# A hybrid retention and attention block: another order of slab products in head pairs 1 to 3

## The reference, cut to what matters

```
h    = rms_norm(x, norm1_g)
proj = h @ w_in                      # 2048 x 7168: rq rk rv rg aq ak av, 8 heads of 128 each
ret  = silu(rg) * group_norm(retention(rotary(rq), rotary(rk), rv))
att  = chunk_attention(rms_norm(aq), rms_norm(ak), av, rel_bias)
x    = x + concat(ret, att) @ w_out  # 2048 x 2048
x    = x + relu(rms_norm(x) @ w_ff1)^2 @ w_ff2      # d_ff = 8192
```

## Time and profile before

| what | value |
|---|---|
| median of 3 runs | 1123.92 us (1123.84 to 1124.09) |
| the profiled execution's own time | 1123.88 us |
| its span, first to last instruction | 1122.1 us |
| PE / DVE / ACT / POOL busy | 98% / 79% / 61% / 5% |
| mean granted TensorE clock | 0.998 |

### The profile page before, as it was taken

The page is one execution under the profiler, slowest core; times in us unless marked ns, Lnnn a source line. Parts: engine busy times, 40 slices in busy tenths (PEclk is TensorE's granted clock), DMA queues, the critical chain, the costliest instruction groups (busy, mean ns, idle before and its releaser), DMA issues.

```text
span 1122.1 us, 13185 instructions
## 1 busy us (share of the span) xinstructions
PE 1104.2 (98%) x5198; PEld 933.7 (83%) x5198; DVE 884.6 (79%) x881; ACT 688.3 (61%) x809; POOL 54.2 (5%) x66
## 2 busy tenths in 40 slices
PE   9799999999999999999999999999999999999998
PEld 9688888988988888888888888888888888888887
DVE  6878777777787768878788778788779788779784
ACT  6565565574565446668756568655667755577652
POOL 0100100100100000000000000000000000000000
PEclk9999999999999999999999999999999999999999
DMA  9785584585576556796797797797787797787792
GB/s 363 261 248 182 156 271 161 166 264 174 169 241 262 187 225 188 230 294 218 233 284 241 249 275 228 230 292 230 262 263 229 247 273 236 257 280 218 246 276 95
DMA packets 42958, 263.81 MB, mean 235 GB/s; under 512 B 4752, under 2 KB 6544, under 8 KB 15120
## 3 DMA queue, kind: packets, MB, share of 16 engines
q1 hardware_dynamic: 36704, 220.22, 52.6%
q0 software_dynamic: 5760, 41.95, 20.3%
q10 hardware_dynamic: 432, 0.81, 0.2%
HBM read 260.85 MB, written 2.10 MB: 234 GB/s over the span
## 4 chain that ended last, share of the span: by engine, by line
PE 85%; DVE 7%; ACT 3%; issue 2%; POOL 1%; ACTq 0%; DVEq 0%
PE acc L869 10%; PE acc L867 10%; PE acc L871 10%; PE acc L739 5%; PE acc L746 5%; PE acc L752 5%; PE bankC L829 4%; PE bankC L824 4%; PE acc L824 4%; PE acc L822 4%; PE bankC L822 4%; PE acc L829 4%; DVE w_lo L1403 3%; PE acc L591 2%; PE acc L596 2%
## 5 line engine op out<-in xcount | busy, mean ns | idle before, releaser
L1690 DVE TENSOR_TENSOR w_lo<-raw,w_hi 128x2048 fp32r<-128x2048 f32 x180 | 410.9, 2288 | 126.9 <-ACT w_hi L1206 126.7
L1206 ACT ACTIVATE w_hi<-raw 128x2048 fp32r<-128x2048 f32 x180 | 344.7, 1916 | 219.5 <-PE acc L871 145.5
L1403 DVE TENSOR_TENSOR w_lo<-raw,w_hi 128x1024 fp32r<-128x1024 f32 (+1 forms) x152 | 167.5, 1106 | 52.4 <-ACT w_hi L993 52.3
L993 ACT ACTIVATE w_hi<-raw 128x1024 fp32r<-128x1024 f32 (+1 forms) x152 | 143.1, 963 | 40.9 <-DVE raw L1412 32.5
L739 PE MATMUL acc<-w_hi,hT_hi 128*128 128x384 f32 (+1 forms) x416 | 105.5, 372 | 0.3 <-ACT w_hi L993 0.2
L867 PE MATMUL acc<-w_hi,hF_hi 128*128 128x512 f32 x256 | 100.8, 394 | 0.0
L871 PE MATMUL acc<-w_hi,hF_lo 128*128 128x512 f32 x256 | 99.7, 390 | 0.0
L869 PE MATMUL acc<-w_lo,hF_hi 128*128 128x512 f32 x256 | 99.7, 389 | 0.0
L746 PE MATMUL acc<-w_hi,hT_lo 128*128 128x384 f32 (+1 forms) x416 | 99.2, 356 | 0.0
L752 PE MATMUL acc<-w_lo,hT_hi 128*128 128x384 f32 (+1 forms) x416 | 98.9, 356 | 0.0
L867 PE MATMUL acc<-w_hi,dF_hi 128*128 128x512 f32 x248 | 96.9, 391 | 0.0
(11 more groups left out here) (262 smaller groups left out, 1813.8 us busy)
## 6 DMA issues: line engine op xcount, KB each, us to landing
raw<-in_w_up SPq DMA_DIRECT2D x64, 1024.0 KB, 6.2
raw<-in_w_down SPq DMA_DIRECT2D x64, 1024.0 KB, 6.1
raw<-in_w_ret SPq DMA_DIRECT2D x32, 1024.0 KB, 5.3
raw<-in_w_att SPq DMA_DIRECT2D x28, 768.0 KB, 4.2
raw<-in_w_out SPq DMA_DIRECT2D x16, 1024.0 KB, 4.9
raw<-in_w_up POOLq DMA_DIRECT2D x16, 1024.0 KB, 8.9
raw<-in_w_down POOLq DMA_DIRECT2D x16, 1024.0 KB, 8.6
raw<-in_w_ret POOLq DMA_DIRECT2D x8, 1024.0 KB, 8.5
```

Source lines behind the costliest of these rows:

```text
L993: nc.scalar.activation(piece(w_hi, q, 0, n), raw[:, r, half * n:(half + 1) * n], ACT.Copy).then_inc(hi_done, 1)
L1206: nc.scalar.activation(w_hi[:, ring(s)], raw[:, r, :], ACT.Copy).then_inc(slab_hi, 1)
L1403: nc.vector.tensor_tensor(piece(w_lo, q, 0, n), raw[:, IN_PLAN[i, READ_AT.get(step, step)][0], half * n:(half + 1) * n], piece(w_hi, q, 0, ...
L1690: nc.vector.tensor_tensor(w_lo[:, ring(s)], raw[:, r, :], w_hi[:, ring(s)].bitcast(f32), ALU.subtract).then_inc(slab_lo, 1)
```

## The change

Blocks 1 to 3 get another order of steps; block 0 keeps its order but some positions move; the x forms are made earlier on DVE; the first weight sum is put in front of the attention norm, on DVE and in POOL's queue; set_w no longer waits for set_y, but set_y for set_w. In order of pieces, blocks 1 to 3 after have I0 0-1, I1 2-3, I2 4-5, Q1 6-7, I3 8-9, J0 10-11, P5 12-13, J1 14-15, P6 16-17, J2 18-19, P7 20-21, J3 22-23, P3 24-25, and from Z1 on as before. No arithmetic is added or removed.

```diff
-STEPS = "I0 I1 I2 I3 J0 Q1 J1 P5 J2 P6 J3 P7 P3 Z1 Q2 Z2 P4 H1 H2".split()
-LOADS = "I0 I1 I2 I3 J0 a J1 b J2 d J3 Z1 e Z2 H1 H2".split()
+FIRST_STEPS = "I0 I1 I2 I3 J0 Q1 J1 P5 J2 P6 J3 P7 P3 Z1 Q2 Z2 P4 H1 H2".split()
+FIRST_LOADS = "I0 I1 I2 I3 J0 a J1 b J2 d J3 Z1 e Z2 H1 H2".split()
+STEPS = "I0 I1 I2 Q1 I3 J0 P5 J1 P6 J2 P7 J3 P3 Z1 Q2 Z2 P4 H1 H2".split()
+LOADS = "I0 I1 I2 a b I3 J0 d J1 J2 J3 Z1 e Z2 H1 H2".split()
...
+        def steps(i):
+            return STEPS if i else FIRST_STEPS
...
POOL:
-                att_power(2 * i)
                 pool.wait_ge(in_summed, 2 * i + 1)
                 add_ret(i, "b", 1, 1, in_b, i)
+                att_power(2 * i)
...
PE (att_T, att_scores, att_PT, att_pv):
-                for h, places in ((2 * i, (13, 15, 19, 21)), (2 * i + 1, (27, 28, 31, 33))):
+                first = (13, 15, 20, 22), (27, 28, 31, 33)
+                rest = (14, 16, 20, 22), (28, 30, 33, 34)
+                for h, places in zip((2 * i, 2 * i + 1), rest if i else first):
...
-                at_piece(i + 1, 5 if late else 7, ret_ZT, 2 * i + 1)
+                at_piece(i + 1, 5 if late else 8, ret_ZT, 2 * i + 1)
...
ACT:
             def set_y(i):
-                act.wait_ge(piece_used, in_first(i, "P7") + 2)
+                act.wait_ge(w_set, i + 1)
...
+                b = int(i > 0)
+                if b:
+                    at_piece(i, 8, keep_in_q1, i)
+                at_piece(i, (8, 10)[b], att_proj, h)
+                at_piece(i, (9, 11)[b], att_squares, h)
+                if not b:
+                    at_piece(i, 12, keep_in_q1, i)
+                at_piece(i, (16, 14)[b], keep_in_p5, i)
+                at_piece(i, (13, 14)[b], att_qT, h)
                 at_piece(i, 17, att_exp, h)
-                at_piece(i, 19, att_pT, h)
-                at_piece(i, 21, att_mix, h)
-                at_piece(i, 22, att_proj, h + 1)
-                at_piece(i, 23, set_y, i)
-                at_piece(i, 24, att_squares, h + 1)
-                at_piece(i, 25, set_h, i)
+                at_piece(i, 20, att_pT, h)
+                at_piece(i, 22, att_mix, h)
+                at_piece(i, (22, 24)[b], att_proj, h + 1)
+                at_piece(i, 24, set_y, i)
+                at_piece(i, (24, 25)[b], att_squares, h + 1)
+                at_piece(i, (25, 26)[b], set_h, i)
...
-                at_piece(i + 1, 4 if late else 6, ret_scale, u + 1)
-                at_piece(i + 1, 5 if late else 7, ret_mix, u + 1)
+                at_piece(i + 1, 4 if late else 7, ret_scale, u + 1)
+                at_piece(i + 1, 5 if late else 8, ret_mix, u + 1)
...
DVE:
             def set_w(i):
-                dve.wait_ge(y_set, i + 1)
+                dve.wait_ge(piece_used, in_first(i, "P7") + 2)
...
+            for pos, b in ((3, 1), (4, 3), (5, 0), (6, 2)):
+                at_piece(0, pos, s_first, b)
+            at_piece(0, PIECES - 1, s_second)
             at_piece(0, PIECES - 1, x_mean_squares)
-            at_piece(0, PIECES - 1, s_first)
-            at_piece(0, 8, s_second)
-            at_piece(0, 10, s_lo, 0)
-            at_piece(0, 12, s_third)
-            at_piece(0, 13, s_lo, 1)
-            at_piece(0, 16, s_lo, 2)
-            at_piece(0, 17, s_lo, 3)
+            at_piece(0, 8, s_third)
+            for f, pos in enumerate((9, 12, 15, 18)):
+                at_piece(0, pos, s_lo, f)
...
-                at_piece(i, 10, att_mean_squares, h)
-                at_piece(i, 11, att_norm, h)
-                at_piece(i, 11, in_sum, i, "b", "Q1")
-                at_piece(i, 13, att_kT, h)
-                at_piece(i, 14, in_sum, i, "d", "P5")
-                at_piece(i, 15, att_bias_max, h)
+                at_piece(i, (10, 8)[b], in_sum, i, "b", "Q1")
+                at_piece(i, (14, 12)[b], in_sum, i, "d", "P5")
+                at_piece(i, (10, 12)[b], att_mean_squares, h)
+                at_piece(i, (11, 13)[b], att_norm, h)
+                at_piece(i, (13, 14)[b], att_kT, h)
+                at_piece(i, (15, 16)[b], att_bias_max, h)
                 at_piece(i, 18, att_probs, h)
-                at_piece(i, 20, set_z, i)
-                at_piece(i, 21, att_mix, h)
-                at_piece(i, 23, set_w, i)
+                at_piece(i, (20, 19)[b], set_z, i)
+                at_piece(i, 22, att_mix, h)
+                at_piece(i, (24, 22)[b], set_w, i)
...
-                at_piece(i + 1, 0 if late else 1, ret_rotate, u + 1)
-                at_piece(i + 1, 0 if late else 2, ret_rotated, u + 1)
+                at_piece(i + 1, 0, ret_rotate, u + 1)
+                at_piece(i + 1, 0 if late else 1, ret_rotated, u + 1)
...
```

More of the change, by code:

```diff
@@ L349, in hybrid_block @@
         PLAN = raw_plan()
+        def steps(i):
+            return STEPS if i else FIRST_STEPS
         def in_slab(i, step):
-            return len(STEPS) * i + STEPS.index(step)
+            return len(STEPS) * i + steps(i).index(step)
         def in_first(i, step):
@@ L360, in in_plan @@
             for i in range(BLOCKS):
-                for name in LOADS:
+                for name in LOADS if i else FIRST_LOADS:
                     r = min(free, key=lambda r: free[r])
@@ L374, in in_step @@
             i, n = divmod(s, len(STEPS))
-            return i, STEPS[n], half
+            return i, steps(i)[n], half
         def in_cols(step):
@@ L467, in _ @@
                     load_in(0, "J0")
-            for name in LOADS[5:8]:
+            for name in FIRST_LOADS[5:8]:
                 load_in(0, name)
             sp.dma_start(bias[:], rel_windows).then_inc(bias_in, 16)
-            load_in(0, LOADS[8])
+            load_in(0, FIRST_LOADS[8])
             sp.dma_start(cosb[:], rope_cos.rearrange("(m p) d -> p m d", p=P)).then_inc(rope_in, 16)
@@ L476, in _ @@
             load_decay(1)
-            for name in LOADS[9:]:
+            for name in FIRST_LOADS[9:]:
                 load_in(0, name)
@@ L1143, in _ @@
                 h, u, late = 2 * i, 2 * i, i == BLOCKS - 1
[L1144 to L1148, removed]
-                at_piece(i, 17, att_exp, h)
-                at_piece(i, 19, att_pT, h)
-                at_piece(i, 21, att_mix, h)
-                at_piece(i, 22, att_proj, h + 1)
-                at_piece(i, 23, set_y, i)
-                at_piece(i, 24, att_squares, h + 1)
-                at_piece(i, 25, set_h, i)
[L1156 to L1160, removed]
+                b = int(i > 0)
[7 more added lines that the diff above has]
+                at_piece(i, (13, 14)[b], att_qT, h)
+                at_piece(i, 17, att_exp, h)
+                at_piece(i, 20, att_pT, h)
[4 more added lines that the diff above has]
+                at_piece(i, (25, 26)[b], set_h, i)
+                at_piece(i, (27, 28)[b], att_qT, h + 1)
+                at_piece(i, (29, 31)[b], att_exp, h + 1)
+                if b:
+                    at_piece(i, 32, ret_proj, u)
+                    at_piece(i, 33, att_pT, h + 1)
+                    at_piece(i, 34, att_mix, h + 1)
+                else:
+                    at_piece(i, 31, att_pT, h + 1)
+                    at_piece(i, 32, ret_proj, u)
+                    at_piece(i, 33, att_mix, h + 1)
                 at_piece(i, 34, ret_exp, u)
@@ L1433, in s_block, with s_first @@
                                         hT_lo[:, tiles, tile_cols(m)].bitcast(f32), ALU.add).then_inc(s_blk_ok, 1)
[L1435 to L1440, removed]
+            def s_first(b):
+                dve.wait_ge(xc_hi, SLAB_KT)
+                dve.wait_ge(xc_lo, SLAB_KT)
+                s_block(b)
             def s_mix_of(f, a, b, op, after):
@@ L1452, in s_second @@
             def s_second():
+                dve.wait_ge(s_blk_ok, 4)
                 s_mix_of(0, s_blk[:, 1, :], s_blk[:, 3, :], ALU.subtract, 0)
@@ L1629, in _ @@
-            at_piece(0, 17, s_lo, 3)
+            at_piece(0, 8, s_third)
+            for f, pos in enumerate((9, 12, 15, 18)):
+                at_piece(0, pos, s_lo, f)
             for i in range(BLOCKS):
                 h, u, late = 2 * i, 2 * i, i == BLOCKS - 1
-                at_piece(i, 10, att_mean_squares, h)
-                at_piece(i, 11, att_norm, h)
-                at_piece(i, 11, in_sum, i, "b", "Q1")
-                at_piece(i, 13, att_kT, h)
-                at_piece(i, 14, in_sum, i, "d", "P5")
-                at_piece(i, 15, att_bias_max, h)
-                at_piece(i, 18, att_probs, h)
-                at_piece(i, 20, set_z, i)
-                at_piece(i, 21, att_mix, h)
-                at_piece(i, 23, set_w, i)
[L1642 to L1646, removed]
+                b = int(i > 0)
+                at_piece(i, (10, 8)[b], in_sum, i, "b", "Q1")
[4 more added lines that the diff above has]
+                at_piece(i, (15, 16)[b], att_bias_max, h)
+                at_piece(i, 18, att_probs, h)
+                at_piece(i, (20, 19)[b], set_z, i)
+                at_piece(i, 22, att_mix, h)
+                at_piece(i, (24, 22)[b], set_w, i)
```

(7 more changed lines are left out.)

## The result

The changed kernel takes 1136.18 us (median of 4 runs, 1135.80 to 1136.33) against 1123.99 us for the kernel before beside it: 1.0108 times as long, interval 1.0091 to 1.0126. That is +12.2 us where the prediction had +5.7, and outside its range. The profiled span is 1134.4 us.

What follows compares the result with a forecast made beforehand. PE, busy 98% of the span, was taken as the bound, so only its waits and slow clock could move. Terms +4.2 (blocks 1 to 3), -1.9 (block 0), +3.4 (clock) gave +5.7: 1129.6 us, range 1121.0 to 1133.5.

Steps and rivals of the forecast that it cites:

- the two waits: Blocks 1 to 3, new PE waits: att_T for a_qk, 2.8 to 2.9 us; P7 for set_z, 1.8 us.
- the clock: Behind att_T's new waits in blocks 1 to 3: two falls taken at 1.7 each, +3.4 us; bounds 0 to 5.1.
- rival 2: Blocks 1 to 3: a_qk reaches PE in time, att_T's wait mostly absent; faster, down to 1117.5 us; chance 0.2.
- The waits in blocks 1 to 3: New waits cost 4.8 us per block, removed waits of r_qk, P5 and P6 give 3.4: +1.4 each, +4.2.
- Block 0: First block: removed slow stretch and a_p wait, less a later J1 and two Z1 waits: -1.9 us; bounds -5.7 to +1.0.
- the two large terms: Block 0: slow-clock stretch behind P5's w_hi wait gone, -1.7 us; att_PT's wait for a_p gone, -1.4 us.
- the two Z1 terms: Block 0: set_w behind a w_lo makes Z1 wait 0.8 us, and w_hi behind att_squares 0.4 us.
- The term for the slow stretch: Block 0, behind P5's w_hi wait: 3.5 us at about half clock, taken as gone with the change, -1.7 us.
- The upper bound of +1.0: Block 0's worst case: the clock falls all the same and the two Z1 waits stay, +1.0 us.
- Rival 1: Blocks 1 to 3: same new waits but the clock stays up, +2.3 us, 1126.2 us; chance 0.3.
- Rival 3: P5 and P6 keep their waits because loads come late: +3.4 us more per block, near 1136 us; chance 0.05.
- Rival 4: New and old waits just cancel: 1124 us; chance 0.12.

Runs made afterwards that it cites:

- ms_first: Changed kernel with att_mean_squares in front of the second weight sum on DVE, both at piece 12: 1132.77 us, ratio 1.0071 to the kernel before.
- rest_only: Changed kernel with block 0 put back in the order of before, blocks 1 to 3 as changed: 1134.95 us, ratio 1.0089 to the kernel before.
- experiment 3: Also written set_z_17: changed kernel with set_z at piece 17 instead of 19 in blocks 1 to 3: 1126.98 us, ratio 1.0024 to the kernel before.
- block0_only: Changed kernel with only block 0 as changed, blocks 1 to 3 in the order of before: 1124.01 us, ratio 1.000 to the kernel before.
- sumb_ms: Changed kernel with the first weight sum one piece earlier (blocks 1 to 3) and att_mean_squares before the second sum: 1124.21 us, ratio 1.0004.

## Why the prediction was wrong

**The sign and the two waits were right.** The measured +12.2 is +5.9 from the waits in blocks 1 to 3, +6.3 from the clock and 0 from block 0, for +4.2, +3.4 and -1.9. The new waits stand where they were said to be, with the releasers that were named: a_qk 2.82 us for "2.8 to 2.9", set_z 1.78 to 1.81 for 1.8. Those of r_qk, P5 and a_p in blocks 1 to 3 are gone.

**Step that failed most: the clock, +3.4 forecast, 6.3 measured.** Three things were wrong in it. The first is the limit, taken from the two waits of the earlier trace rows: 2.6 us fell, 1.4 did not, and so only att_T's 2.85 was put down as able to bring the clock down, and rival 2 said that 2.0 would not, "as 2.0 is nearer to 1.4". A wait of 1.81 us (block 3) and one of 1.79 (ms_first) did. The set_z waits were thus left out as places where it can fall. The second is the number of falls, two of three: the profiled execution has three, one per block. The third is the price. 1.7 was that of the one stretch in the earlier trace rows; blocks 2 and 3 cost 1.7 each, but in block 1 the clock stayed at the lower level for 6.8 us (131.70 to 138.50, granted clock 0.50), 6.0 of them busy, and that cost 2.8. The bound of "three (3 x 1.7 = 5.1)" was therefore too low.

The prediction set beside this the rule of the Trainium skill (TensorE: Matmul & The Clock Gate, section on the HAM clock gate), that the monitor runs free of the kernel, and held against it that the runs of before show no spread. These runs agree with the rule: 2.82 us of idle brought the clock down in blocks 1 and 2 of the changed kernel, not in its block 3, nor in blocks 1 and 2 of rest_only; and runs of one kernel lie 1.3 to 2.1 us apart, or 3.4 to 3.9. The narrow spread of the kernel before was no evidence against it, because a fall in its block 0 does not reach its time. Beside the experiments that kernel ran 40 times: 28 runs have a mean granted clock of 0.997 or 0.998, as the profiled one with its one fall, and 12 have 1.000, as without one. The medians of the two kinds are 1124.07 and 1124.14 us.

**The waits in blocks 1 to 3, +4.2 forecast, +5.9 measured.** The mechanism was right, and the terms were each a little off. att_T costs 2.99 from start to start for 2.85 + 0.1. set_z costs 1.96 (experiment 3) for 1.75 + 0.1. att_PT of the second head, where 0.2 was named and costed at nothing, comes 0.2 us late in block 1 (175.91 for 175.68, by the steps of the rows in front of it). What went away is then 2.99 + 1.96 + 0.2 - 1.97 = 3.2 for 3.4. Together this is 0.6 us a block.

**Block 0, -1.9 forecast, +0.2 in the trace and 0.0 alone.** From P5 to P3 the two large terms came as said: 19.8 us (42.48 to 62.32) for 22.9 before (41.48 to 64.35), 3.0 less for 1.7 + 1.4, with the clock at 1.00. But P5 itself starts 1.0 us later, where it was to start "at about the same time as now", and from P3 to the second head's att_T block 0 loses 2.2 where the two Z1 terms made 1.2, as set_w, w_hi and a_qk are late one behind the other. The term for the slow stretch was wrong in another way too: whether the kernel before has that fall or not, its time is the same, as shown above, so its removal could not be counted as 1.7 off the total. And the fall is not gone for good: in the traces of block0_only and set_z_17 it comes some 8 us earlier, behind the wait at Q1's second piece, again at no price. The prediction had no term for att_T of the second head in block 0; it waits 0.49. The upper bound of +1.0 is also not the sum of the two waits it names, 0.8 + 0.4 = 1.2.

a_qk's power is listed with 1.38 us (39.73 to 41.11), of which the first 0.31 lie under the issue of the DMA before it, and DVE idle throughout. By the rule of the Trainium skill on the shared SBUF interfaces (GPSIMD Engine Reference, 1. Specifications) it was to take 1.03; it ends 1.07 behind the DMA's issue, so the trace agrees with that and not with 1.64. But the same was not asked of the other power: rstd1's took 1.02 before, beside s_block, and 1.75 after, beside a w_lo, because the x forms in front of it moved it there. J1 starts 1.66 us later instead of 0.6.

**The rivals.** Rival 1 (the clock stays up) would have been 1126.2, and without falls the kernel takes 1129.9: it is wrong both in the clock and in the waits. Rival 2 (a_qk in time) did not occur in this kernel. sumb_ms is nearest to it: its blocks give 0.5 each where the rival had 1.5, with 0.3 us of the wait left, and the total stays even, as the clock falls at the other wait. Rival 3 (old waits stay) is excluded by the rows: PE waits neither at P5 nor at P6. That its 1136 is the measured time is luck; its own terms, 3.4 more per block on 1129.6, would make 1139.8. Rival 4 (cancel) is excluded.

What stays open is what decides whether a given wait brings the clock down, why a fall lasts about 3.4 us in two blocks and 6.8 in another, and whether block 1 loses longer in every execution. Why a fall in block 0 of the kernel before costs nothing is not shown either; there is no trace of it without the fall.

## What to carry to other kernels

When an order of steps is changed in queues written by hand, take the gain as given only when the late operation that comes next has been moved as well. Here an order that lost 12 us became one that won 8 by moving three VectorE entries by two pieces or less, and 11 with two more. On PE, a wait of 1.8 to 2.8 us in front of dense work cost itself here and up to about as much again in clock; where it can't be taken away, matmuls without use in its place can give the second part back (6.3 us here). But count a fall only where PE has no wait behind it that swallows it: in block 0 falls came and went without changing the time. And a spread of runs in steps of one size is a sign that the clock falls in some executions and not in others.

## What the runs showed of the hardware

- The clock fell behind idle times of PE of 1.8 us, and did not behind others of 2.82. One fall cost 1.5 to 1.7 us in blocks 1 to 3, once 2.8, and nothing in block 0.
- What a small power on POOL takes depends on whether DVE is inside an instruction with two SBUF operands when the power starts, and on how much of it is left. In the 13 traces this holds for 55 powers without exception: a power of 128x2 ends 0.57 or 0.58 us after the end of that DVE instruction, one of 128x4 0.86 to 0.91 after it. So it took 1.02 us beside a 128x512 s_block or s_mix, 1.47 to 1.78 beside a w_lo, and 3.00 beside the weight sum of 128x2048. All others took 0.69 to 0.71 us (128x2) or 1.03 to 1.04 (128x4), and 1.37 or 1.38 right behind a DMA issue. A w_lo that starts after the power, be it by 0.08 us, does not slow it, in the changed kernel:

```profile
161.94 1.03 POOL L539 TENSOR_TENSOR a_rs<-a_ms,neg_half 128x4 f32<-128x4 f32 x1 [24.39 <-DVE a_ms L1494]
162.02 1.23 DVE L1419 TENSOR_TENSOR w_lo<-raw,w_hi 128x1024 fp32r<-128x1024 f32 x1 [0.17 <-ACT w_hi L1000]
```
